# The third unit of a projection joins the first two behind three norms

## The reference

```python
mod = silu(c) @ w_ada + b_ada
sh1, sc1, g1, sh2, sc2, g2 = split(mod, 6)
u = rmsnorm(h, norm1_w) * (1.0 + sc1) + sh1      # norm 0 (layer 1), norm 2 (layer 2)
h = h + g1 * mixer(u)                            # HGRN2 and differential attention; NSA and stick-breaking
u = rmsnorm(h, norm2_w) * (1.0 + sc2) + sh2      # norm 1 (layer 1), norm 3 (layer 2)
h = h + g2 * ((silu(u @ w_gate) * (u @ w_up)) @ w_down)    # 2816 wide
```

## Time and profile before

| | us |
|---|---|
| median of 3 runs | 1480.11 (1479.55 to 1480.24) |
| profiled execution | 1478.87 |
| its span | 1476.7 |
| TensorE busy | 1441.3 (98%) |
| VectorE busy | 940.1 (64%) |
| ScalarE busy | 411.9 (28%) |
| GpSimd busy | 94.7 (6%) |

### The profile page before, as it was taken

The page is one execution under the profiler, slowest core; times in us unless marked ns, Lnnn a source line. Parts: engine busy times, 40 slices in busy tenths (PEclk is TensorE's granted clock), DMA queues, the critical chain, the costliest instruction groups (busy, mean ns, idle before and its releaser), DMA issues.

```text
span 1476.7 us, 19358 instructions
## 1 busy us (share of the span) xinstructions
PE 1441.3 (98%) x7210; PEld 1170.4 (79%) x7210; DVE 940.1 (64%) x1669; ACT 411.9 (28%) x836; POOL 94.7 (6%) x75
## 2 busy tenths in 40 slices
PE   6999999999999999999999999999999999999997
PEld 4888776778888888888877777788887888888886
DVE  8788697876667665656566668865555444444343
ACT  5434464231111110103244455511122222221011
POOL 0100000200000000325200000000020000000110
PEclk9999999999999999999999999999999999999999
DMA  9253322435655655433221111122222223223332
GB/s 370 112 180 131 132 103 93 143 128 185 204 190 190 198 182 158 148 98 115 72 71 58 43 44 44 51 93 100 101 85 86 99 88 108 88 99 93 93 94 92
DMA packets 52608, 175.78 MB, mean 119 GB/s; under 512 B 5952, under 2 KB 6336, under 8 KB 52544
## 3 DMA queue, kind: packets, MB, share of 16 engines
q1 hardware_dynamic: 52544, 174.94, 34.9%
HBM read 172.82 MB, written 2.10 MB: 118 GB/s over the span
## 4 chain that ended last, share of the span: by engine, by line
PE 91%; DVE 5%; ACT 2%; issue 1%; DMA 0%; POOL 0%; ACTq 0%; DVEq 0%
PE bank L664 20%; PE bank L665 20%; PE bank L666 20%; PE bank L1159 7%; PE bank L1179 2%; PE bank L1013 2%; PE bank L1214 2%; PE bank L1190 2%; PE bank L840 2%; PE bank L838 2%; PE bank L839 2%; PE bank L872 1%; DVE wl L1710 1%; PE bank L676 1%; PE bank L678 1%
## 5 line engine op out<-in xcount | busy, mean ns | idle before, releaser
L664 PE MATMUL bank<-uh,wh 128*128 128x512 f32 x808 | 316.1, 391 | 4.8 <-DVE wl L1710 3.6
L665 PE MATMUL bank<-ul,wh 128*128 128x512 f32 x808 | 315.3, 390 | 0.0
L666 PE MATMUL bank<-uh,wl 128*128 128x512 f32 x808 | 315.2, 390 | 0.0
L1708 DVE CAST wh<-wraw 128x1024 fp32r<-128x1024 f32 (+1 forms) x223 | 148.2, 665 | 194.2 <-PE bank L666 177.1
L1710 DVE TENSOR_TENSOR wl<-wraw,wh 128x1024 fp32r<-128x1024 f32 (+1 forms) x223 | 260.6, 1169 | 7.7
L664 PEld LDWEIGHTS bank<-uh,wh 128*128 128x128 f32 x808 | 152.1, 188 | 37.5 <-issue 4.9
L666 PEld LDWEIGHTS bank<-uh,wl 128*128 128x128 f32 x808 | 152.2, 188 | 31.5
L665 PEld LDWEIGHTS bank<-ul,wh 128*128 128x128 f32 x808 | 152.2, 188 | 31.3
L664 PE MATMUL bank<-hh,wh 128*128 128x512 f32 x352 | 137.6, 391 | 0.0
L666 PE MATMUL bank<-hh,wl 128*128 128x512 f32 x352 | 137.2, 390 | 0.0
L665 PE MATMUL bank<-hl,wh 128*128 128x512 f32 x352 | 137.1, 389 | 0.0
(11 more groups left out here) (352 smaller groups left out, 2258.2 us busy)
## 6 DMA issues: line engine op xcount, KB each, us to landing
ada<-in_w_ada_dram SPq DMA_DIRECT2D x96, 512.0 KB, 4.5
wraw<-in_w_in_dram SPq DMA_DIRECT2D x61, 512.0 KB, 3.2
wraw<-in_w_ffn_gate_dram SPq DMA_DIRECT2D x44, 512.0 KB, 3.2
wraw<-in_w_ffn_up_dram SPq DMA_DIRECT2D x44, 512.0 KB, 3.2
wraw<-in_w_ffn_down_dram SPq DMA_DIRECT2D x32, 512.0 KB, 3.4
wraw<-in_w_ffn_down_dram SPq DMA_DIRECT2D x16, 384.0 KB, 3.1
wraw<-in_w_out_dram SPq DMA_DIRECT2D x16, 256.0 KB, 2.8
wraw<-in_w_out_dram SPq DMA_DIRECT2D x8, 512.0 KB, 3.2
```

The lines of the kernel that those rows point to most:

```text
L664: nc.tensor.matmul(bank[:], a, rh[:, k0 + k, :], start=(first and k == 0), stop=False)
L665: nc.tensor.matmul(bank[:], a, rl[:, k0 + k, :], start=False, stop=False)
L666: mm = nc.tensor.matmul(bank[:], b, rh[:, k0 + k, :], start=False, stop=(last and k == nk - 1))
L1708: V.tensor_copy(wh[:, slot, 0:n], wraw[:, slot, 0:n]).then_inc(w_hi, 1)
```

## The change

Behind norms 1, 2 and 3 three units are multiplied where two were. The third unit's weights are split by VectorE into wxh and wxl, places of their own in memory that is free at that time, so that the split doesn't wait for the first unit: the cast at the start of `norm_u`, the subtraction behind tile 1's ul. In a pair, the two matmuls on uh of each unit stand ahead of the two on ul and wait for uh alone. The filler behind the spread goes from 10 to 5 (norm 1) and 6 (norms 2 and 3). In the ffn phases the second gate unit is read from bank 2, the split of the second up unit stands ahead of hf of iteration 0, and the two modulations that stood ahead of that hf stand behind its hl. Behind norm 2 the third unit is qa2's first, so r_sum's matmuls stand behind it; qa2's second unit goes to bank 3 and its split stands ahead of VectorE's wait for r_std.

```diff
@@ memory
+        x_at = [r_at + 16 * K2, r_at, r_at + 28 * K2]
+        wxh = [at(f"wxh{n}", [P, KT * P], F32R, where=w) for n, w in enumerate(x_at)]
+        wxl = [at(f"wxl{n}", [P, KT * P], F32R, where=w + 2 * K2) for n, w in enumerate(x_at)]
@@ TensorE: passes_both becomes passes_three
+            def passes_three(ph, banks, n, n_before):
+                slots = take(ph, 0, 0), take(ph, 0, 1)
+                def pair(k):
+                    pe.wait_ge(n_uh, n_before + k + 1)
+                    for bank, slot in zip(banks, slots):
+                        a = wh[:, slot, k * P:(k + 1) * P]
+                        b = wl[:, slot, k * P:(k + 1) * P]
+                        nc.tensor.matmul(bank[:], a, uh[:, k, :], start=(k == 0), stop=False)
+                        nc.tensor.matmul(bank[:], b, uh[:, k, :], start=False, stop=False)
                     pe.wait_ge(n_ul, n_before + k + 1)
                     for bank, slot in zip(banks, slots):
                         a = wh[:, slot, k * P:(k + 1) * P]
+                        mm = nc.tensor.matmul(bank[:], a, ul[:, k, :], start=False, stop=(k == KT - 1))
                         if k == KT - 1:
                             mm.then_inc(unit_done, 1)
+                def third(k):
+                    if k == 0:
+                        pe.wait_ge(w_split, ph.u0 + 3)
+                    a, b = wxh[n][:, k * P:(k + 1) * P], wxl[n][:, k * P:(k + 1) * P]
+                    nc.tensor.matmul(B[2][:], a, uh[:, k, :], start=(k == 0), stop=False)
+                    nc.tensor.matmul(B[2][:], a, ul[:, k, :], start=False, stop=False)
+                    mm = nc.tensor.matmul(B[2][:], b, uh[:, k, :], start=False, stop=(k == KT - 1))
+                    if k == KT - 1:
+                        mm.then_inc(unit_done, 1)
+                pair(0)
+                pair(1)
+                third(0)
+                third(1)
+                for k in (2, 3):
+                    pair(k)
+                    third(k)
+                for k in range(4, KT):
+                    pair(k)
+                for k in range(4, KT):
+                    third(k)
@@ TensorE: ffn, body of an iteration as before
+                pe.wait_ge(drain_a, ph.a0)
+                pe.wait_ge(h_ok, h0)
+                passes_three(ph, (B[0], B[1]), n, n_before)
+                up(1)
+                over(pe, name, body, part=(2, ph.iters))
@@ TensorE: norm 1; norm 3 alike with 6; norm 2
-            keep_busy(10, B[2])
-            ffn("ff1", KT, H1)
+            keep_busy(5, B[2])
+            ffn("ff1", 0, KT, H1)
...
-            keep_busy(10, B[2])
-            simple("kc2", uh, ul, 2 * KT)
+            keep_busy(6, B[2])
+            pe.wait_ge(drain_a, PH["kc2"].a0)
+            passes_three(PH["kc2"], (B[PH["kc2"].u0 % 2], B[(PH["kc2"].u0 + 1) % 2]), 1, 2 * KT)
             pe.wait_ge(ssr_ok, 7)
...
-            simple("qa2", uh, ul, part=(0, 1))
+            passes(B[3], take(PH["qa2"], 0, 1), KT, uh, ul, 0, True, True)
@@ VectorE
+            def third_hi(u, n):
+                v.wait_ge(w_in[u % 2], 16 * (u // 2 + 1 - FRONT // 2))
+                V.tensor_copy(wxh[n][:], wraw[:, u % 2, :]).then_inc(w_hi, 1)
+            def third_lo(u, n):
+                v.wait_ge(w_hi, u + 1)
+                V.tensor_tensor(wxl[n][:], wraw[:, u % 2, :], wxh[n][:].bitcast(F32), ALU.subtract).then_inc(w_split, 1)
             def norm_u(nu, shift):
+                u = PH[("ff1", "kc2", "ff2")[nu - 1]].u0 + 2
+                third_hi(u, nu - 1)
...
+                    if t == 2:
+                        third_lo(u, nu - 1)
@@ VectorE: ffn
-                body(0, begun=True)
+                ahead(ph, 1, 0)
+                body(0, begun=2)
+                for j in MOD_AFTER.get(ph.u0 + 2, ()):
+                    modulation(j)
+                body(1, begun=1)
@@ VectorE: behind norm 2
-            ahead(PH["kc2"], 0, 1)
+            ahead(PH["qa2"], 0, 0)
             v.wait_ge(r_std, 1)
             V.reciprocal(rcolr, stdr).then_inc(r_col, 1)
-            ahead(PH["qa2"], 0, 0)
```

More of the change, by code:

```diff
@@ L685, in take, with simple @@
                 return (ph.u0 + c) % 2
-            def simple(name, rh, rl, n_before=None, part=None):
+            def simple(name, rh, rl, part=None):
                 ph = PH[name]
                 def body(i):
[L692 to L701, removed]
+                    for c in range(2):
+                        slot = take(ph, i, c)
+                        pe.wait_ge(drain_a, i * 2 + (ph.a0 + c - 1))
+                        passes(B[(ph.u0 + c) % 2], slot, KT, rh, rl, 0, True, True)
+                over(pe, name, body, part=part)
             def out_proj(name, rh, rl, ready):
@@ L714, in out_proj, with ffn, up @@
                 over(pe, name, body, peel=True)
-            def ffn(name, n_before, h0):
+            def ffn(name, n, n_before, h0):
                 ph = PH[name]
+                def up(i):
+                    slot = take(ph, i, 1)
+                    pe.wait_ge(h_ok, i + h0)
+                    passes(B[1], slot, KT, uh, ul, 0, True, True)
                 def body(i):
[L720 to L732, removed]
+                    slot = take(ph, i, 0)
+                    pe.wait_ge(drain_a, i + ph.a0)
+                    passes(B[0], slot, KT, uh, ul, 0, True, True)
+                    up(i)
+                pe.wait_ge(drain_a, ph.a0)
[3 more added lines that the diff above has]
+                over(pe, name, body, part=(2, ph.iters))
             def turn_out(k):
@@ L1360, in ffn, with body @@
                 ph = PH[name]
-                def body(i):
+                def body(i, bank=B[0]):
                     act.wait_ge(unit_done, i * 2 + (ph.u0 + 1) + U1)
-                    A(sg[:, 0], B[0][:], ACT.Silu).then_inc(drain_a, 1)
+                    A(sg[:, 0], bank[:], ACT.Silu).then_inc(drain_a, 1)
                     act.wait_ge(h_ok, i + (base + H1 + 1))
                     A(hh[:, ds(i, 1), :].rearrange("p a t -> p (a t)"), hf[:, 0], ACT.Copy).then_inc(hh_ok, 1)
-                over(act, name, body)
+                body(0)
+                body(1, B[2])
+                over(act, name, body, part=(2, ph.iters))
             act.wait_ge(c_land[0], 16)
@@ L1549, in _ @@
             A(stdr, B[6][:, 0:NT], ACT.Sqrt, bias=epst).then_inc(r_std, 1)
-            drain("qa2", qa, 0, ACT.Copy, part=(0, 1))
+            for c in range(2):
+                act.wait_ge(unit_done, PH["qa2"].u0 + c + 1 + U1)
+                A(qa[:, c, :], B[2 + c][:], ACT.Copy).then_inc(drain_a, 1)
             for n in range(2):
@@ L1818, in ffn, with body @@
                 ph = PH[name]
-                def body(i, begun=False):
-                    if not begun:
+                def body(i, begun=0):
+                    if begun < 1:
                         ahead(ph, i, 0)
-                    ahead(ph, i, 1)
+                    if begun < 2:
+                        ahead(ph, i, 1)
                     v.wait_ge(unit_done, i * 2 + (ph.u0 + 2) + U1)
@@ L1830, in body @@
                                     ALU.subtract).then_inc(hl_ok, 1)
-                body(0, begun=True)
+                ahead(ph, 1, 0)
[3 more added lines that the diff above has]
+                body(1, begun=1)
                 if name == "ff1":
-                    for i in range(1, ph.iters):
+                    for i in range(2, ph.iters):
                         body(i)
                 else:
-                    loop(ph, body, (1, ph.iters))
+                    loop(ph, body, (2, ph.iters))
             sv = [0]
```

10 lines of the change are left out of this document (2 added, 8 removed).

## The result

The changed kernel takes 1482.19 us (median of 20 runs, 1481.08 to 1483.53), the kernel before on the same chip 1479.51 us (20 runs, 1478.04 to 1480.24). The ratio is 1.0018 [1.0012, 1.0024]: 2.7 us slower. That lies within the range given, and a little under the 3.0 us that I took for the least that can be told from no change. With 20 runs of each it can be told: the interval doesn't reach 1, and the fastest run of the change is slower than the slowest of before. I forecast no change (-0.05 us). The profiled execution of the changed kernel took 1481.24 us (span 1479.5).

What follows compares the result with a forecast made beforehand. TensorE, busy 1441.3 of 1476.7 us, was taken as the bound. Norm 1 -2.1, norm 3 -1.95 and norm 2 +4.0 sum to -0.05 us on the median of 1480.11: forecast 1480.1 us, range 1476.6 to 1483.4.

Steps and rivals of the forecast that it cites:

- Norm 1: Behind norm 1: earlier pair, no stall after it, small waits at later units; -2.1 us, bounds -1.5 and -2.7.
- Norm 3: Behind norm 3: pair 0.8 us earlier, old stall gone, 0.5 wait for third_lo; -1.95 us, bounds -2.2 and -1.0.
- Norm 2, front: Behind norm 2: TensorE reaches the first compression matmul at 694.9 instead of 697.87, 3.0 us won.
- Norm 2, late release: Compression: later r_sum starts GpSimd's 18.9 us chain late, next unit starts at 708.1; +2.7 us, bounds +1.5 and +4.2.
- Norm 2, low clock: Behind the wait for GpSimd in norm 2: six matmuls at low clock; +1.3 us, bounds 0 and 3.
- The first rival: Norm 2: GpSimd's chain keeps 20.3 us (+4.2), clock stays low longer (+2.0); +2.2, 1482.3 us; chance 0.22.
- The sum: Whole kernel: -2.1 - 1.95 + 4.0 = -0.05 us, forecast 1480.1 us.

Runs made afterwards that it cites:

- g1: The changed kernel with 4 and 17 filler matmuls ahead of TensorE's first and second wait for wfin: 1477.27 us, ratio 0.9990.
- f3: The change at norm 2 alone, norms 1 and 3 as in the kernel before: 1486.13 us, ratio 1.0046.
- g3: f1 with GpSimd waiting for VectorE's split of qa2's second unit between its first product and first add: 1475.91 us, ratio 0.9974.
- g4: The kernel before with r_sum behind qa2's first unit and the split of qa2's second unit ahead of VectorE's wait for r_std: 1488.10 us, ratio 1.0064.
- f1: The changed kernel with r_sum moved ahead of the pair behind norm 2, replacing four of six fillers: 1475.39 us, ratio 0.9972.
- f2: The change at norms 1 and 3 alone, norm 2 as in the kernel before: 1474.73 us, ratio 0.9970.
- g2: The changed kernel with GpSimd's work on the compression weights cut to 8 of 128 columns, position terms left out: 1472.16 us, ratio 0.9952.
- h1: g3 with six filler matmuls ahead of TensorE's second wait for wfin: 1473.65 us, ratio 0.9962.
- h3: The kernel before with uh matmuls ahead of ul in ffn's pairs and filler 5 and 6 at norms 1 and 3: 1479.29 us, ratio 0.9998.
- h4: f2 with the pair in the old order, waiting for ul, and filler 10: 1475.04 us, ratio 0.9971.

## Why the prediction was wrong, step by step

**Norm 1, -2.1 forecast.** Right: cast in the idle stretch, pair 2.4 us behind the spread, no stall after the pair. The small waits were 0.2, 0.1 and 0.7 (at 319.27, 324.92, 331.18) instead of 0.2, 0.4 and 0.9, and one of 0.35 for wxl came where none was forecast. Measured -2.7 against the trace I predicted from, -1.67 against the two traces of before without the low stretch at norm 1. My forecast took that stretch for a part of the kernel, before and after; only some executions have it.

**Norm 3, -1.95.** Right: -1.7 and -1.77; the wait for wxl was 0.35, not 0.5.

**Norm 2, front, -3.0.** Right: -2.9 (29.28 to 26.37).

**Norm 2, late release, +2.7.** Right in mechanism, 0.4 short in size. r_sum started 19.55 us behind the spread (19.3 forecast), GpSimd 1.08 behind it (1.04), the chain took 705.92 - 687.17 = 18.75 us (18.9). But from its end to the next unit went 0.50 us and not 0.2, 0.2 of it because the one-column matmuls between stand at the low clock (39.88 against g1's 39.67). The first unit came 39.88 us behind the spread, before 705.38 - 668.59 = 36.79: +3.1.

**Norm 2, low clock, +1.3.** This is the step that failed. I took six slow matmuls from the restart near 239 us. The clock was back at 241.9 there, 2.9 us behind the restart; here it stayed low to 710.4, 4.0 us behind the next unit's start. From the first unit to hc it was 12.87 against 716.37 - 705.38 = 10.99 us: +1.9, and 13.1 in the second trace (low to 710.8): +2.1. With the 0.2 in the release the low clock costs 2.1 to 2.3 us, which g1 shows by taking it away. The mistake was to price a wait by one restart of another kind: the clock did not fall with the long wait, it fell 1.9 us ahead of it (at 700.2, the wait begins at 702.0). In the records every trace with an unfilled wait for wfin in the compression has the low level there (after twice, f3 twice, g3, g4, for 7 to 14 us). In all but g3 a first wait of 0.56 us ends 0.1 to 3.0 us ahead of the fall; in g3 the fall lies inside its single wait of 1.38. None of the traces in which the same 62-column matmuls ran without such a wait or with it filled has it (before three times, f1, f2, g2, g1 twice, h1, h3, h4). Norm 2 in all: +5.0 in the first pair of traces, +5.3 in the last, forecast +4.0, and -2.1 - 1.95 could not cover that.

The first rival (+4.2 and +2.0, 1482.3) had this term right. Its chain of 20.3 us did not happen, but its low clock of 2.0 did, and its condition was met: late release and low clock together came to 3.1 + 2.1 = 5.2, past the 4.05 that the other norms were to bring. I gave it 0.22. That its time is so near the measured one is in part luck: it stands on the same terms for norms 1 and 3, and on a longer chain.

**The sum.** -1.67 - 1.77 + 5.33 = +1.9 in the last pair of traces, where -0.05 was forecast. Of these 1.9 us the low clock brings 0.8, the late release 0.5, norm 1 0.4 and norm 3 0.2: the low clock is the largest, not the only one. The medians give +2.7. Both traces of the change lie at the low end of its runs (1481.24 and 1481.17, where 20 runs gave 1481.08 to 1483.53), so the 0.8 us between +1.9 and +2.7 are in no trace and stay unexplained.

The Trainium skill ("TensorE: Matmul & The Clock Gate", Part 1) says that the gate's phase isn't tied to the kernel's start, and that the same kernel therefore measures different numbers of slow matmuls. The traces agree: those at norm 1 and at the scores come and go between executions of before (368.45 or 369.51, 21.18 or 22.75). By that rule neither was fit to be a term of the sum.

**Open.** Whether the low stretch in the scores belongs in part to the late release. With before's order of norm 2 scores-kd was 21.1 or 21.2 in two traces, 22.8 in three and 24.3 in one; with the late, unfilled wait 22.7 in three and 24.4 in two; with it filled or the chain short 21.2 in three of three, but with r_sum first 22.7 in three of three. f3's median, 7.0 us over before where its stages of norm 2 give 4.4 to 5.3, leaves 1.6 to 2.6 us over, which speaks for it; that before and f2 show the stretch too speaks against. Open as well is which wait brings the clock down, since no run fills only the first or only the second.

## What to carry to other kernels

Before a small reduction is moved behind a larger block, follow what it releases on the engines that look idle: GpSimd was busy for 6% of the span, and its 18.75 us chain, with 1.0 us to spare, set the time. The price of the wait on TensorE had two terms here, the lateness and the clock behind it, and filler ahead of the wait took away the second (2.1 to 2.3 us in g1, 3.1 in h1) where it could not touch the first. The stall at a hand-over between units went when another unit's work stood there; starting the first earlier mostly moved it (0.8 us earlier, 0.46 more wait).

## What was not expected of the hardware

- A wait of 0.56 us among 62-column matmuls stood ahead of a stretch of 10 to 14 us at 1.2 GHz in five traces (a longer wait followed inside it), and in g3 one of 1.38 us held the start of a stretch of 7 us; the same matmuls without a wait kept 2.4 GHz, and so they did in g1, where 0.83 us of the wait were left behind 4 us of filler.
- A low stretch that covered another wait cost 0.1 us: in the first trace of before the clock is low from 685.6 to 689.0 and n2-cmp is 29.28, in the others it is at its full level there and TensorE waits 1.2 us for wl: 29.18.
- GpSimd and VectorE's splits hold each other up in both directions: a cast of 0.69 us took 2.82 beside GpSimd's adds, a subtraction of 1.22 took 2.17, and three adds took 5.74 (f1); with the split let through first (g3) they took 0.69, 1.22 and 4.58.
